# Weights split in two halves, and a feed-forward stage fed from the undivided residual, in one step of a hybrid decoder

## The reference

```python
def rmsnorm(x, g):
    y = x32 * lax.rsqrt(jnp.mean(x32 * x32, axis=-1, keepdims=True) + EPS) * g
def conv_ffn(h, w_up, conv_w, conv_b, w_down, conv_hist):
    u = jnp.einsum('btd,df->btf', h, w_up)
    u_ctx = jnp.concatenate([conv_hist, u], axis=1)
    c = conv_b + sum(conv_w[i] * u_ctx[:, i:i + T] for i in range(3))
    gate, val = jnp.split(c, 2, axis=-1)
    y = jnp.einsum('btf,fd->btd', jax.nn.gelu(gate) * val, w_down)
...
    x = x + rmsnorm(cross_attn(rmsnorm(x, n_x_pre), mem_kv, w_xq, w_xo), n_x_post)
    y, new_conv = conv_ffn(rmsnorm(x, n_ffn_pre), w_up, conv_w, conv_b, w_down, conv_hist)
    x = x + rmsnorm(y, n_ffn_post)
```

## Time and profile before

| | us |
|---|---|
| median of 3 runs | 2705.14 (2703.39 to 2705.47) |
| the profiled execution | 2697.52 |
| its span, first to last instruction | 2695.9 |
| TensorE busy | 2595.8 (96%) |
| VectorE busy | 1549.1 (57%) |
| ScalarE busy | 1233.5 (46%) |
| TensorE's granted clock, mean | 0.985 |

### The profile page before, as it was taken

One profiled execution on the slowest core, in us unless ns is written; L12 is line 12 of the kernel. 1 busy time (PEld: TensorE's weight loads), 2 busy tenths in 40 slices (PEclk: granted clock), 3 DMA queues, 4 the chain that ended last, 5 costly groups with the idle time before them and its releaser, 6 DMA issues. The chain is left out here.

```text
span 2695.9 us, 52549 instructions
## 1 busy us (share of the span) xinstructions
PE 2595.8 (96%) x20839; PEld 2500.5 (93%) x20839; DVE 1549.1 (57%) x1943; ACT 1233.5 (46%) x1551; POOL 196.6 (7%) x307
## 2 busy tenths in 40 slices
PE   7999999999999999999999999998999999999997
PEld 5988888999999999999999988888899999999997
DVE  4556455444555555545644556455766665666666
ACT  5455554433443444433333534334555555455553
POOL 1111112000111111100000001310000000000000
PEclk9999999999999999999999999999999999999999
DMA  6778779666888888866657745855366567666563
GB/s 197 219 243 251 233 234 297 177 178 176 233 235 235 234 234 233 222 175 191 172 160 210 210 125 174 275 177 173 101 180 179 164 183 201 179 177 178 164 182 114
DMA packets 855041, 530.81 MB, mean 197 GB/s; under 512 B 13961, under 2 KB 832065, under 8 KB 854135
## 3 DMA queue, kind: packets, MB, share of 16 engines
q1 hardware_dynamic: 822583, 440.07, 59.4%
q0 software_dynamic: 27312, 86.50, 9.3%
q10 hardware_dynamic: 5032, 2.62, 0.3%
HBM read 499.79 MB, written 33.29 MB: 198 GB/s over the span
## 5 line engine op out<-in xcount | busy, mean ns | idle before, releaser
L520 DVE TENSOR_TENSOR weights_lo<-weights_raw,weights_hi 128x2048 fp32r<-128x2048 f32 x407 | 932.2, 2291 | 763.9 <-ACT weights_hi L513 762.0
L544 PE MATMUL bank<-h_hi,weights_hi 128*128 128x264 f32 x4624 | 1335.7, 289 | 18.9 <-DVE h_lo L2542 11.4
L545 PE MATMUL bank<-h_lo,weights_hi 128*128 128x264 f32 x4624 | 1316.6, 285 | 0.0
L546 PE MATMUL bank<-h_hi,weights_lo 128*128 128x264 f32 x4624 | 1315.1, 284 | 0.0
L544 PEld LDWEIGHTS bank<-h_hi,weights_hi 128*128 128x128 f32 x4624 | 876.6, 190 | 36.8 <-issue 22.8
L545 PEld LDWEIGHTS bank<-h_lo,weights_hi 128*128 128x128 f32 x4624 | 877.8, 190 | 2.0 <-issue 1.9
L513 ACT ACTIVATE weights_hi<-weights_raw 128x2048 fp32r<-128x2048 f32 x407 | 777.2, 1910 | 216.8 <-PE bank L546 207.2
L546 PEld LDWEIGHTS bank<-h_hi,weights_lo 128*128 128x128 f32 x4624 | 873.3, 189 | 0.0
L544 PE MATMUL bank<-y_hi,weights_hi 128*128 128x264 f32 x1232 | 353.5, 287 | 7.4 <-DVE y_lo L2450 3.8
L546 PE MATMUL bank<-y_hi,weights_lo 128*128 128x264 f32 x1232 | 352.1, 286 | 0.0
L545 PE MATMUL bank<-y_lo,weights_hi 128*128 128x264 f32 x1232 | 350.6, 285 | 0.0
(11 more groups left out here) (377 smaller groups left out, 2213.3 us busy)
## 6 DMA issues: line engine op xcount, KB each, us to landing
weights_raw<-in_w_in SPq DMA_DIRECT2D x177, 1024.0 KB, 7.0
weights_raw<-in_w_up SPq DMA_DIRECT2D x88, 1024.0 KB, 5.9
weights_raw<-in_w_down SPq DMA_DIRECT2D x64, 704.0 KB, 4.8
gla_state_sample<-in_state_gla POOLq DMA_DIRECT2D x32, 512.0 KB, 6.6
out_gla_s<-gla_state_sample POOLq DMA_DIRECT2D x32, 512.0 KB, 6.5
weights_raw<-in_w_br_gla SPq DMA_DIRECT2D x16, 1024.0 KB, 5.9
weights_raw<-in_w_mix_out SPq DMA_DIRECT2D x16, 1024.0 KB, 5.8
weights_raw<-in_w_xkv SPq DMA_DIRECT2D x16, 1024.0 KB, 6.0
```

Source lines behind the costliest of these rows:

```text
L520: nc.vector.tensor_tensor(w_lo[:, r, :], raw[:, r, :], w_hi[:, r, :].bitcast(F32), ALU.subtract).then_inc(lo_ready, 1)
L544: nc.tensor.matmul(out, wh, xh, start=first and n == 0, stop=False)
L545: nc.tensor.matmul(out, wh, xl, start=False, stop=False)
L546: mm = nc.tensor.matmul(out, wl, xh, start=False, stop=last and n == len(blocks) - 1)
```

## The change

**Halves.** Every pass over a weight slot, high and low, becomes two passes over 1024 columns, eight blocks each. `hi_ready` and `lo_ready` count halves. The low part of the first half waits only for the high part of the first half. TensorE starts a slot when its first half is ready and waits once more at its ninth block. The transfer still waits for the whole slot.

**The norm before the feed-forward** is written anew. The gain after cross-attention is put on when tiles are copied to `merged`. VectorE works in rounds of two tiles: times root, add to the residual, and with a lag of one round h_lo. h_hi and h_lo are made of the residual times the gain, undivided. The squares of the residual go to nine buffers (`square(t)`: three of `squares`, three of `ffn_gate`, three of `ffn_value`) and are summed by TensorE with 32 columns of ones into four quarters of bank 7; one more matmul adds the quarters. TensorE runs slots 0 and 1 of the up-projection block by block side by side, the sums five blocks behind, and slot 2 ten blocks behind. The turns of the history stand ahead of the last cross-attention product, and the split of the last slot's successor stands inside the norm. The other norm at its place, n = 0, keeps its form.

**Division at emptying.** Each up-projection tile is multiplied by the reciprocal root on VectorE, from PSUM into one of the three `squares` buffers; this frees the bank. ScalarE and the taps read the buffer. The split of weights moves from the end of `conv` to behind this product, for the slot before.

```diff
+        def square(t):
+
+            return (sqr, cg, cv)[t % 9 // 3][:, t % 3, :]
...
-            nc.scalar.activation(w_hi[:, r, :], raw[:, r, :], ACT.Copy).then_inc(hi_ready, 1)
+            for half in HALVES:
+                nc.scalar.activation(w_hi[:, r, half], raw[:, r, half], ACT.Copy).then_inc(hi_ready, 1)
 
         def split_lo(dve, p, j, i=0, ahead=RING):
 
             r = p.s(j + ahead)
-            dve.wait_ge(hi_ready, p.c(j, i) + RING + 1)
             dve.wait_ge(projected, p.c(j, i) + 1)
-            nc.vector.tensor_tensor(w_lo[:, r, :], raw[:, r, :], w_hi[:, r, :].bitcast(F32),
-                                    ALU.subtract).then_inc(lo_ready, 1)
+            for n, half in enumerate(HALVES):
+                dve.wait_ge(hi_ready, p.c(j, i) * 2 + (2 * RING + 1 + n))
+                nc.vector.tensor_tensor(w_lo[:, r, half], raw[:, r, half], w_hi[:, r, half].bitcast(F32),
+                                        ALU.subtract).then_inc(lo_ready, 1)
...
-            sp.wait_ge(lo_ready, p.c(j, i) + 1)
+            sp.wait_ge(lo_ready, p.c(j, i) * 2 + 2)
...
-                pe.wait_ge(lo_ready, p.c(j, i) + RING + 1)
+                pe.wait_ge(lo_ready, p.c(j, i) * 2 + (2 * RING + 1))
+            second = [n for n, b in enumerate(blocks) if b[0] >= SLOT // 2 and (fresh or b[0] == SLOT // 2)][:1]
...
+                if n in second:
+                    pe.wait_ge(lo_ready, p.c(j, i) * 2 + (2 * RING + 2))
...
-                copy(merged[:, ds(n, 1), :], out[:, None, :])
+                nc.scalar.activation(merged[:, ds(n, 1), :], out[:, None, :], ACT.Copy, scale=scale)
...
+                if j == 0:
+                    split_hi(act, PH_XO_E, j)
+            act.wait_ge(*V_N[1].at("var"))
+            nc.scalar.activation(rstd[:, :], rstd[:, :], ACT.Sqrt).then_inc(A_N[1]("root"), 1)
+            split_hi(act, PH_XO_E, 1)
+
+            def squares(c):
+                for t in (2 * c, 2 * c + 1):
+                    if t >= 9:
+                        act.wait_ge(*P_N[1].at(f"s{t - 9}"))
+                    nc.scalar.activation(square(t), xres[:, t, :], ACT.Square).then_inc(A_N[1](f"q{t}"), 1)
+            for c in range(8):
+                act.wait_ge(*V_N[1].at(f"x{c}"))
+                for t in (2 * c, 2 * c + 1):
+                    nc.scalar.activation(h_hi[:, t, :], xres[:, t, :], ACT.Copy, scale=param(PC_FPRE, t))\
+                        .then_inc(A_N[1](f"hi{t}"), 1)
+                if c:
+                    squares(c - 1)
+            squares(7)
+            act.wait_ge(*V_N[1].at("var2"))
+            nc.scalar.activation(rstd[:, :], rstd[:, :], ACT.Sqrt).then_inc(A_N[1]("root2"), 1)
...
+                    if hi_first:
+                        split_hi(act, p, j, i)
                     if kind:
-                        act.wait_ge(*p.saved(j - 1, i))
+                        act.wait_ge(*V.at(f"u{j - 1}", i))
                         g = cg[:, q, :]
                         nc.scalar.activation(g, g, ACT.Gelu_apprx_tanh).then_inc(S(f"g{q}"), 1)
-                    act.wait_ge(projected, p.c(j, i) + 1)
                     if V is V_F[half]:
                         before = V.at(f"lo{q}", i - 1)
                     else:
                         before = V_F[half].at("lo0", 6)
                     act.wait_ge(*before)
+                    act.wait_ge(*p.saved(j, i))
                     c = (cg, cv)[kind][:, q, :]
-                    nc.scalar.activation(c, bank[p.outs[j]][:, 0:T], ACT.Identity, scale=param(PC_CW + 176 + col, n),
+                    nc.scalar.activation(c, sqr[:, j % 3, :], ACT.Identity, scale=param(PC_CW + 176 + col, n),
...
+                    if not hi_first:
+                        split_hi(act, p, j, i)
+                for j in range(6):
+                    conv(up, A_F[half], V_F[half], j, 0, j // 2, half == 0 and j < 2)
...
+            xo_slot(PH_XO_E, 0, 0)
             pe.wait_ge(hr_in, 16)
             for c in range(4):
                 for r in range(4):
                     mm = turn(bank[3 + c][:, r * 2 * FT:(r + 1) * 2 * FT], hrows[:, 4 * c + r, :], 2 * FT)
                 mm.then_inc(P_H(f"h{c}"), 1)
-            norm_sums(1)
+            xo_slot(PH_XO_E, 1, 0)
+            norm(1, V_OUT["xo_end"].at("acc3"))
+
+            def square_sum(t):
+                r = 32 * (t % 4)
+                pe.wait_ge(*A_N[1].at(f"q{t}"))
+                nc.tensor.matmul(bank[7][r:r + 32, 0:T], ones[:, 0:32], square(t), start=t < 4, stop=t >= KB - 4)\
+                    .then_inc(P_N[1](f"s{t}"), 1)
+
+            def up_block(j, n):
+                return product(pe, PH_FFN[0][0], j, j, 0, [H_BLOCKS[n]], fresh=n == 0, first=n == 0, last=n == KB - 1)
+            LAG = 10
+            pe.wait_ge(*V_N[1].at("var"))
+            for n in range(KB):
+                pe.wait_ge(*V_N[1].at(f"lo{n}"))
+                for j in range(2):
+                    mm = up_block(j, n)
+                    if n == KB - 1:
+                        mm.then_inc(projected, 1)
+                if n >= 5:
+                    square_sum(n - 5)
+                if n >= LAG:
+                    up_block(2, n - LAG)
+            for t in range(KB - 5, KB):
+                square_sum(t)
+            for n in range(KB - LAG, KB):
+                if n == KB - LAG + 2:
+                    pe.wait_ge(*V_N[1].at("four"))
+                    nc.tensor.matmul(bank[7][:, 0:T], ones[:, :], acc[:, :], start=True, stop=True).then_inc(P_N[1]("all"), 1)
+                mm = up_block(2, n)
+            mm.then_inc(projected, 1)
             for half, (up, up_e, down, down_e) in enumerate(PH_FFN):
-                with pe.Fori(0, 7) as i:
+                for j in range(0 if half else 3, 6):
...
+            xo_slot(PH_XO_E, "xo_end", 0, 0)
             dve.wait_ge(mem_out[2], 16)
...
+            xo_slot(PH_XO_E, "xo_end", 1, 0)
+            V1 = V_N[1]
+            dve.wait_ge(*P_N[1].at("sum"))
+            nc.vector.tensor_scalar(rstd[:, :], bank[7][:, 0:T], 1.0 / D, EPS, ALU.mult, ALU.add).then_inc(V1("var"), 1)
+            dve.wait_ge(*A_N[1].at("root"))
+            nc.vector.reciprocal(rstd[:, :], rstd[:, :]).then_inc(V1("rstd"), 1)
+            dve.wait_ge(*V1.at("rstd"))
+
+            def low(c):
+                for t in (2 * c, 2 * c + 1):
+                    dve.wait_ge(*A_N[1].at(f"hi{t}"))
+                    nc.vector.scalar_tensor_tensor(out=h_lo[:, t, :], in0=xres[:, t, :], scalar=param(PC_FPRE, t),
+                                                   in1=h_hi[:, t, :].bitcast(F32), op0=ALU.mult, op1=ALU.subtract)\
+                        .then_inc(V1(f"lo{t}"), 1)
+            for c in range(8):
+                m, x = merged[:, 2 * c:2 * c + 2, :], xres[:, 2 * c:2 * c + 2, :]
+                nc.vector.tensor_tensor(m, m, rstd[:, None, :].to_broadcast([P, 2, T]), ALU.mult).then_inc(V1(f"yr{c}"), 1)
+                if c:
+                    low(c - 1)
+                dve.wait_ge(*V1.at(f"yr{c}"))
+                nc.vector.tensor_tensor(x, x, m, ALU.add).then_inc(V1(f"x{c}"), 1)
+                if c == 3:
+                    split_lo(dve, PH_XO_E, 1)
+            low(7)
+            dve.wait_ge(*P_N[1].at("s15"))
+            nc.vector.tensor_copy(acc[:, :], bank[7][:, 0:T]).then_inc(V1("four"), 1)
+            dve.wait_ge(*P_N[1].at("all"))
+            nc.vector.tensor_scalar(rstd[:, :], bank[7][:, 0:T], 1.0 / (32 * D), EPS, ALU.mult, ALU.add).then_inc(V1("var2"), 1)
+            dve.wait_ge(*A_N[1].at("root2"))
+            nc.vector.reciprocal(rstd[:, :], rstd[:, :]).then_inc(V1("rstd2"), 1)
+            nc.vector.memset(acc[:, :], 0.0).then_inc(V1("zero"), 1)
+            dve.wait_ge(*V1.at("rstd2"))
...
+                    c, u = (cg, cv)[kind][:, q, :], sqr[:, j % 3, :]
+                    dve.wait_ge(projected, p.c(j, i) + 1)
+                    nc.vector.tensor_tensor(u, bank[p.outs[j]][:, 0:T], rstd[:, :], ALU.mult).then_inc(evac[p.outs[j]], 1)
+                    for low in lows:
+                        split_lo(dve, *low)
...
-                    split_lo(dve, p, j, i)
-                with dve.Fori(0, 7) as i:
+
+                for j in range(6):
+                    if half == 0 and j < 3:
+                        lows = [(up, j, 0)] if j < 2 else []
+                    else:
+                        lows = [(up, j - 1, 0)] if j else []
+                    conv(up, A_F[half], V_F[half], j, 0, j // 2, lows)
+                with dve.Fori(1, 7) as i:
                     for j in range(6):
-                        conv(up, A_F[half], V_F[half], j, i, i * 3 + j // 2)
+                        conv(up, A_F[half], V_F[half], j, i, i * 3 + j // 2, [(up, j - 1, i) if j else (up, 5, i - 1)])
                 for j in range(2):
-                    conv(up_e, A_FE[half], V_FE[half], j, 0, 21)
+                    conv(up_e, A_FE[half], V_FE[half], j, 0, 21, [] if j else [(up, 5, 6)])
+                split_lo(dve, up_e, 0)
```

(12 more changed lines are left out.)

80 lines of the change are left out of this document (41 added, 39 removed).

## The result

The changed kernel takes 2681.1 us at the median against 2704.3 of the kernel before in the same comparison: ratio 0.9917, 95% interval 0.9902 to 0.9931. Forecast: 2686, range 2676 to 2700. The profiled execution has a span of 2678.2 us, 17.7 less than before (2695.9). A second comparison gave 0.9935 (0.9920 to 0.9949).

A forecast was written before the change was run, and what follows sets the result against it. TensorE's matrix work was taken as a floor, leaving roughly 100 us of idling and the half-clock time to win. -8.6 + 0.7 + 2.8 - 12 - 2 = -19.1 us from 2705.14 gave 2686, range 2676 to 2700.

The forecast's parts named there:

- The first feed-forward matmul: Sign in the trace: it starts near 1883 less the gains up to there (about 11 us), so near 1872.
- The norm: Before the feed-forward: undivided h and interleaved slots start the fourth up slot earlier; gain 8.6 us, 7.4 to 10.5.
- the price of a sum of squares: On TensorE in the norm: two rows at 0.12 us and 0.2 us for both shape changes, bounds 0 and 0.3.
- Rival C: Norm's sums: shape changes cost 0.5 us per sum and more, 5 to 8 us of gain go; 2692, chance 0.12.
- Halves and clock: Weight passes: fifteen waits each 0.85 us shorter, taken as 12 us, plus 2 us from a half-clock stretch going.
- Rival A: Halves are worth little (4 us), since the next wait takes the time; 2696, chance 0.15.
- the clock, put at 2: Behind waits of 3.60 and 2.81 us: one of two half-clock stretches may go; 2 us, bounds 0 and 5.
- The wait in the down-projection: Second down slot's low part stands behind the last up tile: new 1.4 us wait, twice; cost 2.8, bounds 0 and 5.
- The wait in slot 5: After the norm, VectorE's backlog makes the first low half late for TensorE; cost 0.7 us, bounds 0 and 3.
- Division as tiles are emptied: Up-projection: 88 more VectorE products stay hidden, 9.8 us a pair against TensorE's 11.66, 1.8 left; cost 0.
- Rival D: Up-projections: VectorE becomes the bound, at 12.3 us a pair 28 us lost; 2714, chance 0.08.
- Rival B: Norm: clock stays low through the interleaved blocks, slot 3 starts 1.7 us later than before; 2698, chance 0.14.

The follow-up runs named there:

- edit 2: Changed kernel with sums of squares over 128 columns of ones into one accumulating row set, without the four partial sums: 2676.4 us, 0.9919 of the kernel before.
- Edits 2 and 3: The second of these: changed kernel with its 32-column sums of squares in groups of four, four and eight: 2673.9 us, 0.9911 of the kernel before.
- experiment 1: Kernel before with only the weight passes halved: 2677.8 us, ratio 0.9922; changed kernel with whole passes again: 2702.4 us, 1.0020, both against the kernel before.
- edit 4: Changed kernel with the second down slot's low pass ahead of the last value tile's taps and TensorE's wait at its last block: 2678.0 us, 0.9924 of before.

## Why the prediction held, and where it didn't

Its total, -19.1, stands against -17.7 between the profiled executions, -23.2 between the medians of the first comparison and -17.4 between those of the second. The terms were off by more, to both sides. The first feed-forward matmul came at 1866.3, some 6 us ahead of the place that the prediction named.

**The norm: -8.6 predicted, -3.6 measured** (1921.48 - 1873.91 before, 1900.49 - 1857.90 after, less the 1.38 of turns that moved). The mis-sized term is the price of a sum of squares, "two rows at 0.12 and two changes of shape ... 0.2 us", 0.44 in all; it was 0.76 (1.85 - 1.09). Most of the miss is in the rows: edit 2 shows 0.44 to 0.46 for a sum without any change of shape, so the changes cost 0.3, the prediction's upper bound, and the two rows 0.45 where it took 0.24. The trace of before had that price, at full clock and in this very norm, twelve rows in 2.83 us, 0.222 from one to the next:

```profile
1889.76 2.83 PE L1848 MATMUL bank<-squares,ones 128*128 128x264 f32 x12
```

The step of 0.12 is that of the products of high and low parts. Against the schedule that the prediction computed, with both profiles of the changed kernel:

| from the last cross-attention matmul | predicted | after | lost | after, again |
|---|---|---|---|---|
| first block | 8.0 | 8.4 | 0.4 | 8.4 |
| h_lo of tile 15 ends (VectorE) | 25.1 | 25.6 | | 25.6 |
| tile 6 on TensorE | 16.6 | 16.9 | -0.1 | 16.9 |
| tile 10 | 21.2 | 24.3 | 2.8 | 22.8 |
| tile 15 | 28.9 | 33.7 | 1.7 | 32.2 |
| last squares summed (start of the last row) | 31.7 | 36.3 | -0.2 | 34.8 |
| fourth slot | 37.5 | 42.6 | 0.5 | 41.1 |

VectorE's side was right to half a microsecond over 25. Tiles 10 to 15 lost 1.7, about five times 0.32. Tiles 6 to 10 lost 2.8: four times 0.31 for the sums (a period of 1.48 where a 128-column sum has 1.17), the rest, about 1.6, in the second stretch at half clock (12 matmuls at 0.22). The second profile has no such stretch and is ahead by just that, 1.5; the norm's gain is 5.1 us in it. So of the 5.0 us that were missed about 3 belong to the price of the sums and 1.6 to a stretch of low clock that comes and goes.

Rival C foretold the size, "5 to 8 us of the norm's gain go", but not the mechanism: it had the changes of shape at 0.5 us a sum and more. Its evidence against, was sound for the changes: 0.20 us into the 8-column products and 0.31 out of them, where the lone sum now has 0.21 and 0.32. What it didn't show is the sum's own pace. Edits 2 and 3 show the changes' price directly, by removing it.

**Halves and clock: -14 predicted, -17.4 measured** (16.0 + 1.38). Most single waits are 0.70 to 0.87 shorter where 0.85 was forecast; that part is right. In the heads (of the gated attention, up to about 480 us) a third wait took much of it back. There VectorE's state update waits for ScalarE's, and that for a transfer. Before, first, and after (ScalarE, then TensorE):

```profile
177.71 2.56 ACT L1060 ACTIVATE gla_state_sample<-gla_state_sample,gla_log_decay 128x512 f32<-128x512 f32 x4 [6.22 <-DMA gla_state_sample<-in_state_gla]
...
180.91 1.03 PE L1604 MATMUL bank<-gla_state_sample,gla_q_apart 128*8 128x512 f32 x4 [2.96 <-DVE gla_state_sample L2184]
```

```profile
176.33 2.56 ACT L1079 ACTIVATE gla_state_sample<-gla_state_sample,gla_log_decay 128x512 f32<-128x512 f32 x4 [5.72 <-DMA gla_state_sample<-in_state_gla]
...
180.36 1.03 PE L1648 MATMUL bank<-gla_state_sample,gla_q_apart 128*8 128x512 f32 x2 [4.18 <-DVE gla_state_sample L2253]
```

TensorE arrives 1.78 us earlier and leaves 0.55 us earlier. At 469 us the changed kernel was 2.4 ahead, where the prediction's six places in the heads make 5.1; over the ten profiles with halves the lead at 480 us is 1.2 to 3.8. Rival A, that all places go this way, is refuted by experiment 1.

What made up for it, as far as the traces show, was the clock, put at 2. Near 1364 the wait fell from 2.81 to 2.10, and the low stretch behind it is gone; TensorE before and after, over six us from each restart:

```profile
1364.00:1370.00 6.00, 5.42 (x24) 5.42 (x25) 2.81 (x7) 1.44 (x3) 0.00 (x0) 0.50 0.67 176
```

```profile
1358.40:1364.40 6.00, 4.89 (x38) 4.54 (x39) 4.24 (x11) 3.81 (x7) 0.00 (x0) 1.00 0.65 175
```

Behind the wait 2.7 us were won there, near 1198 0.6, and with the stretch of 6.8 us at 1729 before, absent after, 2 to 3 more around the memory keys, where a wait for a low part (a step of 2.34 us ahead of 1727.32) went too because a weight load landed earlier. How much of this is the halves' and how much chance? The two kernels with whole passes reach the last cross-attention matmul at 1875.3 (turns included) and 1877.2, the nine with halves at 1857.8 in the mean: 18.5 us, so the 17.4 was no lucky pair. That the last 3 to 4 us of it are the clock's is read from traces; no run set the clock apart. Behind the wait near 1364 all ten profiles with halves win: 2.7 us in the five in which the clock stays at 1.00, 1.2 in the five in which it is at 0.50 for 3.4 us, against 6.8 us at 0.50 before. But both groups of five reach the last cross-attention matmul at the same mean, 1857.8 (turns included): what one place gives, others take back.

**The wait in the down-projection: +2.8 predicted, +3.2 measured**, 1.6 twice, at the place and for the reason given; edit 4 removed it. The prediction's sum for it has a slip: its seven terms add up to 5.0 us, not 5.4, which would make the wait 1.0 and the cost 2.1. So the terms were short by 0.6 us a wait, and part of the agreement is luck. The wait in slot 5, put at 0.7, did not show: no step above 0.3 us between the fourth slot's start and 2142.

**Division as tiles are emptied: hidden, as predicted.** VectorE in a pair of up tiles, answering to the earlier trace rows:

```profile
1964.60 0.43 DVE L2769 TENSOR_TENSOR squares<-bank,rstd 128x264 f32<-128x264 f32 x1 [1.76 <-PE bank L564]
...
1969.81 0.43 DVE L2789 TENSOR_TENSOR y_lo<-ffn_value,y_hi 128x264 f32 x1 [0.72 <-ACT y_hi L1125]
1970.40 0.43 DVE L2769 TENSOR_TENSOR squares<-bank,rstd 128x264 f32<-128x264 f32 x1 [0.15 <-PE bank L564]
```

It waits for TensorE 1.76 + 0.15 = 1.9 us a pair; 1.8 was forecast. Rival D falls. Rival B, a clock low all through the interleaved blocks, falls too, but a second stretch of 3.4 us did come in this profile (clock 0.50 from 1876.50 above). It stands behind TensorE's longer idle time at tile 6 (a step of 2.20 us, against 0.98 in the second profile); in the profiles without it the first low stretch lasted longer, so TensorE came to tile 6 with less time to wait.

**The sum by measured terms**: -3.6 + 3.2 - 17.4 = -17.8, against -17.7. The forecast was right by luck in its total: two errors of 5.0 and 3.4 us had opposite signs. And the norm with its division, which most of the change's code is for, is worth next to nothing: 3.6 us won and 3.2 lost to the two new waits here; with whole passes it made the kernel slower (experiment 1).

## What to carry to other kernels

Where VectorE's pass over a tile can only follow ScalarE's, halves of it took about 0.7 us from a wait that ended on that chain, and cost nothing where the engines had slack; where another wait stands close behind, as in the heads, it takes much of that back. Price a small float32 sum between large products in two parts: its own rows, at the pace that rows of its own type show in the trace, and the change of shape there and back. If it uses 32 of 128 columns, issue four into different groups together, or use all 128. And profile the same kernel twice before an edit of 2 us is given a cause: here a stretch of low clock, present in one execution and absent in the next, was worth 1.5.

## What the runs showed of the hardware

- A float32 product of 264 columns shows as two rows, 0.222 us apart at full clock with 128 columns of ones (before and in edit 2), 0.25 apart in a lone sum with 32, while the products of high and low parts step by 0.12.
- Four 32-column sums into four groups start within 0.02 us of each other and put 0.80 us between the products around them; one alone puts 0.78 there, one of 128 columns 0.37 (1884.40 to 1884.77), with a step of 0.32 behind it. Over a whole tile the 32-column sum costs 0.3 us more than the 128-column one.
- Near 1358 us TensorE restarts after a step of 2.4 us in all ten profiles with halves: in five the granted clock stays at 1.00 there, in five it is 0.50 for 3.4 us. After a step of 3.1 us or more, in the two kernels with whole passes, it was 0.50 for 6.8 us both times. At this place a wait shortened by 0.7 us was followed by another 1.2 or 2.7 us won.
- The same code reached the same matmul between 1853.7 and 1863.1 us in nine executions.
